# One k group of every gate chunk pair as seven block products, with sums and copies on the helper engines

## The reference

```
h     = rms_norm(x, mix_pre_gain)
proj  = h @ w_in                       # q, k, v, gm_uv, s5_u, gates
y_a   = stick_breaking_attention(q, k, v) @ w_br_a      # 4 heads of 256
y_b   = spatial_gating(gelu(gm_uv), ...) @ w_br_b       # 4 groups
y_c   = s5_layer(s5_u, ...) @ w_br_c
g     = sigmoid(gates)                 # 3 x 2048 columns
x     = x + rms_norm((g0 * y_a + g1 * y_b + g2 * y_c) @ w_out)
```

## Time and profile before

| | us |
|---|---|
| median of 3 runs (1495.1 to 1496.48) | 1496.4 |
| the profiled execution | 1495.31 |
| its span | 1493.4 |
| TensorE busy (share of the span) | 1482.6 (99%) |
| VectorE busy | 1137.3 (76%) |
| ScalarE busy | 835.3 (56%) |
| GpSimd busy | 151.4 (10%) |

### The profile page before, as it was taken

One profiled execution on the slowest core, in us unless ns is written; L12 is line 12 of the kernel. 1 busy time (PEld: TensorE's weight loads), 2 busy tenths in 40 slices (PEclk: granted clock), 3 DMA queues, 4 the chain that ended last, 5 costly groups with the idle time before them and its releaser, 6 DMA issues.

```text
span 1493.4 us, 19212 instructions
## 1 busy us (share of the span) xinstructions
PE 1482.6 (99%) x6712; PEld 1220.3 (82%) x6712; DVE 1137.3 (76%) x1353; ACT 835.3 (56%) x1018; POOL 151.4 (10%) x286
## 2 busy tenths in 40 slices
PE   9999999999999999999999999999999999999997
PEld 7888887888888888888888888888888888888786
DVE  7878988855454577657576788888888888887897
ACT  7645455565666544656578455555555555555553
POOL 0000000140220000000000222012222221000000
PEclk9999999999999999999999999999999999999999
DMA  9755555666555655856453666766666667656564
GB/s 340 240 189 173 180 183 183 196 201 194 189 185 174 237 180 193 329 196 212 155 197 127 195 207 217 232 218 213 212 211 199 201 208 236 229 173 208 187 208 169
DMA packets 89859, 305.08 MB, mean 204 GB/s; under 512 B 13056, under 2 KB 13568, under 8 KB 88768
## 3 DMA queue, kind: packets, MB, share of 16 engines
q1 hardware_dynamic: 80144, 285.12, 57.8%
q0 software_dynamic: 9216, 18.63, 3.9%
q10 hardware_dynamic: 432, 0.45, 0.1%
HBM read 294.19 MB, written 2.10 MB: 198 GB/s over the span
## 4 chain that ended last, share of the span: by engine, by line
PE 97%; DVE 2%; DMA 0%; ACT 0%; issue 0%; DVEq 0%; POOL 0%; ACTq 0%; POOLq 0%
PE acc L1808 10%; PE acc L1810 10%; PE acc L1809 10%; PE acc L2128 5%; PE acc L2131 5%; PE acc L2130 5%; PE side L2131 5%; PE side L2128 5%; PE side L2130 5%; PE side L1808 4%; PE side L1810 4%; PE side L1809 4%; PE tr L1810 3%; PE tr L1809 3%; PE tr L1808 3%; PE side L2093 1%
## 5 line engine op out<-in xcount | busy, mean ns | idle before, releaser
L548 ACT ACTIVATE w_hi<-raw 128x1024 fp32r<-128x1024 f32 x299 | 314.9, 1060 | 298.4 <-PE acc L2131 91.3
L1001 DVE TENSOR_TENSOR w_lo<-raw,w_hi 128x1024 fp32r<-128x1024 f32 x262 | 320.8, 1227 | 201.5 <-ACT w_hi L529 197.1
L1006 DVE TENSOR_TENSOR w_lo<-raw,w_hi 128x1024 fp32r<-128x1024 f32 x315 | 381.7, 1222 | 105.0 <-ACT w_hi L548 95.4
L529 ACT ACTIVATE w_hi<-raw 128x1024 fp32r<-128x1024 f32 x262 | 276.9, 1059 | 280.8 <-PE acc L1810 165.3
L1808 PE MATMUL acc<-w_hi,xT_hi 128*128 128x512 f32 x504 | 198.3, 393 | 0.1
L1810 PE MATMUL acc<-w_hi,xT_lo 128*128 128x512 f32 x504 | 196.3, 389 | 0.0
L1809 PE MATMUL acc<-w_lo,xT_hi 128*128 128x512 f32 x504 | 196.3, 389 | 0.0
L503 POOL DMA_DIRECT2D hT_st<-h_blk x176 | 93.6, 540 | 492.0 <-DVE h_blk L1073 453.6
L1808 PEld LDWEIGHTS acc<-w_hi,xT_hi 128*128 128x128 f32 x504 | 94.6, 188 | 22.3 <-issue 2.3
L1810 PEld LDWEIGHTS acc<-w_hi,xT_lo 128*128 128x128 f32 x504 | 94.6, 188 | 19.8
L1809 PEld LDWEIGHTS acc<-w_lo,xT_hi 128*128 128x128 f32 x504 | 94.7, 188 | 19.1
(11 more groups left out here) (468 smaller groups left out, 2747.1 us busy)
## 6 DMA issues: line engine op xcount, KB each, us to landing
raw<-in_units SPq DMA_DIRECT2D x530, 512.0 KB, 4.1
hT_st<-h_blk POOLq DMA_DIRECT2D x176, 32.0 KB, 1.8
x_tok<-in_x SPq DMA_DIRECT2D x4, 512.0 KB, 5.7
qkT<-qk_blk POOLq DMA_DIRECT2D x64, 32.0 KB, 2.8
xres<-in_x POOLq DMA_DIRECT2D x1, 2048.0 KB, 9.6
m_raw<-in_mem_t POOLq DMA_DIRECT2D x1, 2048.0 KB, 8.7
mq<-in_mem POOLq DMA_DIRECT2D x1, 2048.0 KB, 15.5
x_raw<-in_x_t SPq DMA_DIRECT2D x6, 256.0 KB, 6.2
```

The lines of the kernel that those rows point to most:

```text
L529: a_.activation(w_hi[:, j % RING], raw[:, j % RING], ACT.Copy).then_inc(hi_ready, 1)
L548: a_.activation(w_hi[:, v % RING], raw[:, slots[block]], ACT.Copy).then_inc(hi_ready, 1)
L1001: v_.tensor_tensor(w_lo[:, s], raw[:, s], w_hi[:, s].bitcast(F32), ALU.subtract).then_inc(lo_ready, 1)
L1006: v_.tensor_tensor(lo[:, v % RING], raw[:, slot], hi[:, v % RING].bitcast(F32), ALU.subtract).then_inc(lo_ready, 1)
```

## The change

It has these parts.

- **Gate stage.** In each head the first group of four k tiles of both chunks becomes seven block products. The head is written out: four plain units of the left chunk, seven products, two plain units of the left chunk, six of the right one: 19 splits in place of 16, from the same 16 loads (`EXTRA` = 12 counts the splits beyond the loads). The four heads are unrolled (`for i in range(HEADS)`).
- **Products.** Three of the results gather in the right chunk's banks `tr`: a product is added to a bank whose partial sum ScalarE has copied out before (`copy_part`, into the gate tiles, for the last head into dead tiles of `proj`). TensorE waits for these copies (`parts_copied`). Finished chunks are no longer taken by ScalarE from PSUM: VectorE adds bank and copy (into `gates`) at steps 13 and 18, and ScalarE applies the Sigmoid in place (`gate_sigmoid`).
- **Slots.** The four blocks fill the four raw slots. The first load behind them waits for the low part of the fifth product, the next two for the sixth, the fourth for the seventh (`head_units`).
- **Side work moves.** Scores behind unit 1 in place of 3, and ScalarE's share of them at step 2 in place of 4; `kT` at 0; the mixing behind product unit 7, the next steps at 11, 13 and 15; on VectorE `sp` at 7, the next head's transposes at 8, and so on. The score matmuls wait for the head before's `ya_lo`.
- **Sums of x.** Once, ahead of the stage, VectorE makes four sums of blocks of x (`X_f`), ScalarE and VectorE split them.
- **Output stage.** The last `hidden_sums` moves from step 61 to 63, its low part from 65 to 67, its high part from 64 to 66; `y3_square` of the second chunk from 57 to 61.

```diff
+def head_units():
...
+    for i in range(HEADS):
+        plain(4)
+        blocks = [load(v + done) for done in (6, 7, 6, 5)]
+        (b11, _), (b12, _), (b21, _), (b22, _) = blocks
...
+        slots += [b22, b21, b11, b12]
+        v += 7
+        plain(8)
+    plain(RING)
@@ SyncE
+            for u, slot, splits in HEAD_LOADS:
+                sp_.wait_ge(lo_ready, splits)
+                sp_.dma_start(raw[:, slot].rearrange("p a b -> p (a b)"), units[u]).then_inc(w_landed[slot], 16)
@@ ScalarE
+            def split_head(v):
+                kind, k, n, slots, landed = HEAD_STEPS[v]
+                block = 0 if kind == "plain" else (0, 0, 2, 0, 3, 0, 1)[k]
+                if kind == "plain" or k in (0, 2, 4):
+                    act.wait_ge(w_landed[slots[block]], landed[block])
+                else:
+                    act.wait_ge(t_ready, 4 * n + {1: 1, 3: 2, 5: 4, 6: 3}[k])
+                act.wait_ge(unit_used, v - (RING - 1))
+                a_.activation(w_hi[:, v % RING], raw[:, slots[block]], ACT.Copy).then_inc(hi_ready, 1)
...
+            def copy_part(i, c, h, src, splits):
+                act.wait_ge(unit_used, U_GATE + HEAD_SPLITS * i + splits)
+                a_.activation(part_of(i, c, h), src, ACT.Copy).then_inc(parts_copied, 1)
...
+            for i in range(HEADS):
+                for j in range(HEAD_SPLITS):
+                    if j == 1 and i:
+                        gate_sigmoid(i - 1, 1)
+                    if j == 0:
                         act.wait_ge(qk_turned, i * 256 + 256)
...
-                    if j == 4:
+                    if j == 2:
                         act.wait_ge(z_done, i + 1)
...
+                    if j == 4:
+                        copy_part(i, 0, 0, tr[:, 1], 5)
+                    if j == 5:
+                        copy_part(i, 1, 1, tr[:, 0], 6)
+                    if j == 7:
+                        copy_part(i, 1, 0, tr[:, 1], 8)
+                    if j == 10:
+                        copy_part(i, 0, 1, tr[:, 1], 11)
+                    if j == 15:
+                        gate_sigmoid(i, 0)
+                    split_head(U_GATE + HEAD_SPLITS * i + j + RING)
...
-                if q in (51, 57, 107):
+                if q in (51, 61, 107):
@@ VectorE
+            def split_head(v):
...
+                if k == 1:
+                    dve.wait_ge(lo_ready, v)
+                    dve.wait_ge(w_landed[b12], landed[1])
+                    difference(b11, b12, b11)
+                if k == 2:
+                    dve.wait_ge(lo_ready, v)
+                    dve.wait_ge(w_landed[b22], landed[3])
+                    difference(b11, b22, b11)
+                if k == 3:
+                    dve.wait_ge(t_ready, 4 * n + 1)
+                    difference(b12, b22, b12)
+                if k == 4:
+                    dve.wait_ge(lo_ready, v)
+                    dve.wait_ge(t_ready, 4 * n + 3)
+                    dve.wait_ge(w_landed[b21], landed[2])
+                    difference(b11, b21, b11)
+                split_at((b11, b11, b21, b11, b22, b11, b12)[k], v)
...
+                    if j in (13, 18):
...
+                            v_.tensor_tensor(gates[:, 2 * i + c, h], bank(3 * c, h), part_of(i, c, h), ALU.add).then_inc(acc_taken[h], 1)
+                    split_head(base + j + RING)
...
-                if q in (3, 5, 20, 61):
-                    hidden_sums((3, 5, 20, 61).index(q))
+                if q in (3, 5, 20, 63):
+                    hidden_sums((3, 5, 20, 63).index(q))
@@ TensorE
-            with pe.Fori(0, 4) as i:
+            for i in range(HEADS):
                 def head_step(j):
-                    if j == 3:
+                    if j == 1:
...
+                        if i:
+                            pe.wait_ge(ya_lo, i)
...
+                for j in range(4):
+                    plain_units(v + j, 1, 0, xT_hi, xT_lo, 4 + UK * j, (g - 1, g - 1) if j == 0 else (None, None))
+                    head_step(j)
...
+                pair_product(v + 4, tr[:, 1], *block_of(xT_hi, xT_lo, 0, 0, 0), True, True, True)
+                pair_product(v + 5, tr[:, 0], *sum_of(X_hi, X_lo, 0), True, True, True)
+                pair_product(v + 6, acc[:, 0], *block_of(xT_hi, xT_lo, 0, 1, 0), False, False)
+                pe.wait_ge(parts_copied, 4 * i + 1)
+                pair_product(v + 7, tr[:, 1], *sum_of(X_hi, X_lo, 1), False, True, True)
+                head_step(7)
+                pe.wait_ge(parts_copied, 4 * i + 2)
+                pair_product(v + 8, tr[:, 0], *sum_of(X_hi, X_lo, 3), False, True, True)
+                pair_product(v + 9, acc[:, 1], *block_of(xT_hi, xT_lo, 0, 1, 1), False, False)
+                pe.wait_ge(parts_copied, 4 * i + 3)
+                pair_product(v + 10, tr[:, 1], *sum_of(X_hi, X_lo, 2), False, True, True)
+                for j in range(2):
+                    plain_units(v + 11 + j, 1, 0, xT_hi, xT_lo, 12 + UK * j, last=(j == 1), full=True)
+                    head_step(11 + j)
+                pe.wait_ge(parts_copied, 4 * i + 4)
+                for j in range(6):
+                    plain_units(v + 13 + j, 1, 3, xT_hi, xT_lo, 4 + UK * j, last=(j == 5), full=True, skip=True)
+                    head_step(13 + j)
```

More of the change, by code:

```diff
@@ L63, with load, plain @@
 FI_SPLITS, FO_SPLITS, FO_LAST = 19, 53, 56
-S_FI, S_FO, S_END = 284, 474, 583
+S_FI, S_FO, S_END = 296, 486, 595
+def head_units():
+    loads, steps = [], {}
+    slots = list(range(RING))
+    free, rounds = [U_GATE - 3 + k for k in range(RING)], [U_GATE // RING] * RING
+    u, v = U_GATE, U_GATE
+    def load(done):
+        nonlocal u
+        s = slots.pop(0)
+        rounds[s] += 1
+        loads.append((u, s, free[s]))
+        free[s], u = done, u + 1
+        return s, rounds[s] * 16
+    def plain(count):
+        nonlocal v
+        for _ in range(count):
+            s, landed = load(v + 1)
+            steps[v] = ("plain", 0, 0, (s,), (landed,))
+            slots.append(s)
+            v += 1
+    for i in range(HEADS):
+        plain(4)
+        blocks = [load(v + done) for done in (6, 7, 6, 5)]
+        (b11, _), (b12, _), (b21, _), (b22, _) = blocks
+        for k in range(7):
+            steps[v + k] = ("pair", k, i, (b11, b12, b21, b22), tuple(landed for _, landed in blocks))
+        slots += [b22, b21, b11, b12]
+        v += 7
+        plain(8)
+    plain(RING)
+    assert slots == list(range(RING)) and v == U_BR + RING and u == v - EXTRA
+    return loads, steps
+HEAD_LOADS, HEAD_STEPS = head_units()
 def late_units():
     loads, steps = [], {}
-    free, rounds = [S_FI - 3 + k for k in range(RING)], [S_FI // RING] * RING
-    slot, pairs = 0, 0
+    free, rounds = [S_FI - 3 + k for k in range(RING)], [(S_FI - EXTRA) // RING] * RING
+    slot, pairs = 0, HEADS
     def load():
@@ L76, in load @@
         rounds[s] += 1
-        loads.append((S_FI + len(loads), s, free[s]))
+        loads.append((S_FI - EXTRA + len(loads), s, free[s]))
         return s, rounds[s] * 16
@@ L2216, with blocks_of @@
     order += [column_chunk(w_in, c * NC) for c in range(8)]
-    order += [gate[11]] + [column_chunk(x["s5_w_glu"], c * NC) for c in range(2)] + gate[:8]
+    order += [gate[11]] + [column_chunk(x["s5_w_glu"], c * NC) for c in range(2)]
+    def blocks_of(left, right, g):
+        tiles = [[part[2 * g:2 * g + 2].reshape(2, P, UK, NC)[:, :, e].transpose(1, 0, 2).reshape(1, P, UK * NC) for e in range(2)]
+                 for part in (left, right)]
+        return [tiles[0][0], tiles[1][0], tiles[1][1], tiles[0][1]]
+    for i in range(HEADS):
+        left, right = gate[2 * i:2 * i + 2]
+        b11, b12, b22, b21 = blocks_of(left, right, 0)
+        order += [left[2:6], b11, b12, b21, b22, left[6:], right[2:]]
     for i in range(4):
@@ L2222 @@
     order += [column_chunk(x["w_xo"], i * NC) for i in range(4)]
-    def blocks_of(left, right, g):
-        tiles = [[part[2 * g:2 * g + 2].reshape(2, P, UK, NC)[:, :, e].transpose(1, 0, 2).reshape(1, P, UK * NC) for e in range(2)]
-                 for part in (left, right)]
-        return [tiles[0][0], tiles[1][0], tiles[1][1], tiles[0][1]]
     for i in range(11):
```

200 lines of the change are left out of this document (121 added, 79 removed).

## The result

| | before | changed |
|---|---|---|
| median of 6 runs each, us | 1495.86 | 1500.61 |
| ratio (95% interval) | | 1.0035 (1.0025 to 1.0045) |
| span of a profiled execution | 1493.4 | 1498.0 |
| TensorE busy | 1482.6 | 1479.5 |
| VectorE busy | 1137.3 | 1183.3 |

The change made the kernel 4.75 us slower (3.7 to 6.7 by the interval), where +5.8 was forecast; the measured 1500.6 lies in the forecast range of 1498.0 to 1507.5. The first thing to read is what TensorE waited for. This is the whole list of the changed kernel (engine, tile and line that waited, what it waited for: us in total, times, longest).

The account below looks back on a forecast made before the run. TensorE, 97% of the last-ending chain, was taken as the bound. Stalls less saved matmuls gave +1.7 us a head, +6.8 for four; the output stage's -1.0 made +5.8, forecast 1502.2 us, range 1498.0 to 1507.5.

Parts of the forecast that it names:

- Six matmuls for each head, 1.36 us: Gate stage, TensorE: 42 matmuls in place of 48 gain 1.36 us a head, 5.4 us for four.
- Average load of the helpers: Per head, VectorE gets 13 us more on 25.8, ScalarE about 5 on 29.3; both fit on average, queue order decides.
- Stalls at unit 7 and unit 8: Fourth and fifth block products: TensorE waits 0.86 and 0.7 us a head for VectorE's low parts.
- Stall at unit 11: First plain unit behind the products: its load waits for a raw slot, stalling TensorE 1.7 us a head.
- sp ends 0.6 before the load lets L11 start: VectorE's four sp operations, 1.6 us, end 0.6 before the load lets unit 11's low part start.
- Bank copies, sums of x, GpSimd's transfers: nothing: Gate stage side work: covered, charged 0; sums up to 2 us if cover were gone, a late copy at most 0.60.
- Table loads: Scores' block on ScalarE: no drain beyond 1.28 us a load; by the skill's page, +11 us on top.
- The output stage, -1.0: Output stage's moved squares and last hidden sums: between 0 and 1.2 us gained, taken as -1.0.
- The lead that covers everything: Rival: the products' lead hides unit 11's load and all gains are kept, 1490.0 us; chance 0.07.
- The second rival: Score block costs nothing, the load does: unit 11 stalls by 0.8, -0.6 a head, 1493.0 us; chance 0.10.
- Late loads: Rival: four block-slot loads issued together land late, +1.8 us a head more, 1509 us; chance 0.09.
- The clock: Rival: TensorE's waits bring the granted clock down to 1.2 GHz, adding 20 us, 1522 us; chance 0.02.

Follow-up runs that it names:

- the Ln: Changed kernel with the scores' Ln, including its table load, put behind the split of unit 6 on ScalarE: 1495.10 us, ratio 0.9997.
- the third difference: Changed kernel with the third weight difference put ahead of unit 6's low part in VectorE's queue: 1496.14 us, ratio 1.0009.
- all together: Changed kernel with unit 11's load in a fifth slot, VectorE's sp later, scores' Ln behind unit 6's split, third difference ahead of unit 6's low part: 1488.94 us.
- the fifth slot alone: Changed kernel with the load of unit 11 sent early to a fifth slot in dead memory: 1498.48 us, ratio 1.0019.
- The doubled copies: Changed kernel with each of the four partial sums per head copied an extra time on ScalarE, into scratch: 1501.42 us, ratio 1.0043.

## Why the prediction was right, point by point

- *Six matmuls for each head, 1.36 us.* Shown: with the waits taken away, a head is 1.31 shorter (46.55 for 47.86).
- *Average load of the helpers is no limit, their order is.* Shown by three runs in which the work is that of the changed kernel and only places differ (the Ln, the third difference, all together). The load itself was put too high: VectorE's busy time in a head rose by 9.9 us and not 13, ScalarE's by 3.4 and not 5; nothing hung on it.
- *Stalls at unit 7 and unit 8, 0.86 and 0.7.* In the second head they cost 0.85 (0.61 + 0.16 + 0.08 for the slow first matmul) and 0.59 (0.35 + 0.24). The first is near by two small errors against each other: I had no term for the slow matmul, and TensorE came to unit 7 0.14 later than drawn (378.43, 10.88 after the scores; I had 10.74). The first head's unit 7 was 0.2 later. The chain ran as drawn: the split of unit 5 started 1.15 after the scores (368.70 against 367.55; I had 1.1), the score copy 2.11 after (I had 2.1), unit 7's low part ended 11.50 after (I had 11.55).
- *Stall at unit 11, 1.7.* Too high: 1.10 + 0.16 + 0.1 = 1.36. Two terms make most of it: the load landed in 3.21 where I had 3.45, and TensorE started unit 8 about 0.15 behind the end of its low part where I had 0.05. I took 0.2 off the head's sum for the landing, so the head came out at +1.7 by the forecast and at +1.5 to +1.75 by the trace; the gate stage's part alone gave +6.5 in place of +6.8.
- *sp ends 0.6 before the load lets L11 start.* The idle time there was 0.38. That this second queue stood just behind the first cause is why the fifth slot alone gave 2.1 and not 5.
- *Bank copies, sums of x, GpSimd's transfers: nothing.* The doubled copies cost 0.1 a head or less where the loads landed in time. The first head, behind the sums of x, began at 312.49 against 312.39 before, and at 312.37 in the run with the third difference moved, which had no wait in its first 40 us. No wait of TensorE in the stage is put down to GpSimd in any run.
- *Table loads.* The next ACTIVATE stands 0.02 behind a load of 1.28 (370.71, 372.01). The Trainium skill, ScalarE: Activation LUTs, "What ACT_TABLE_LOAD costs", adds a drain of 1.38 to each. The trace does not show it, and without both loads the block was 2.4 shorter (4.62 to 2.22), a little less than the two loads' own 2.56. By the figures of the Trainium skill, an estimate, it would have been 5.3 shorter. The measurement decides.
- *The output stage, -1.0.* Too small by the medians: -1.7 by itself, between -0.3 and -3.0 by the interval. I took the two brackets of the earlier trace rows, 0.4 and 0.6, and no more; with 0.16 hidden at each and a slow first matmul they are 1.5, which is what the spans of the two profiled executions differ by (1493.4 and 1491.9). The third wait went in that execution too, but it stayed away when the edit was undone.
- *Rivals.* The lead that covers everything did not exist, and the score block was not free. The second rival's number was tested nearly alone by the run without table loads: it had a stall of 0.8 left at unit 11 and 0.6 a head gained, and the second head shows a bracket of 0.43, about 0.7 in all, and a period of 47.23, 0.6 under that of before. Late loads did not decide: unit 11's landed in 3.2 us in the second and the last head. The loads of the stretch as a whole took longer than before (3.1 to 7.8, median 4.8, against the earlier trace rows), but TensorE waited for none behind unit 11. The clock stayed at its upper level through waits of up to 2 us.

The two errors of size, 0.3 less in the gate stage and 0.7 more from the output stage, have one sign; together they are the 1 us between +5.8 and +4.75. That distance is inside the measurement's own interval of 1.5 us to either side, so the times alone do not prove this account; the waits and periods of the traces carry it. The forecast time of 1502.2 is off by 1.6, and the other half microsecond of it is the kernel before, which was 1496.4 over three runs and 1495.86 over six.

## What to carry to other kernels

A trade of matmuls for helper work was decided here by the longest chain through the helpers' queues at the moment when TensorE takes units fastest, not by their busy share: each product lasts 1.36 us, and a 4.6 us block on ScalarE and a raw slot freed late each cost about 1.4 us a head, each as much as the six matmuls saved. Write down for each in-order queue what stands ahead of the operation that is needed next and does not have to; moving such things on ScalarE and VectorE and giving one load a slot of its own, with no work taken away, turned +4.75 us into -6.6, of which 1.7 is the output stage's edit. Where two causes stand one behind the other (the load and sp), curing the first alone shows only the difference between them: 0.5 us a head of the 1.4 that both together gave.

## What the runs showed of the hardware

The bracket of idle time understates a wait for a low part by about 0.25 us at this matmul form: 0.16 of overlap with the matmul before and 0.1 in which the first matmul behind the wait is slow (379.20 has 0.47 for 0.39). Three waits of up to 1.2 us in each 49 us, and a single one of 2.00, did not bring the granted clock down: 1.00 in either stretch, 0.999 or 0.998 over each profiled execution. A 512 KB load that started alone landed in 3.21 us, the low end of the earlier trace rows; in one head of one run it took 4.1, cause not found.
